# A fourteen-stage transformer block on one Trainium2 core: token-major first tiles behind nine layer norms, a bias table through DRAM, and one tile for three small projections

## What is computed

| j | 0 | 1 | 2 | 3 | 4 | 5 | 6 | 7 | 8 | 9 | 10 | 11 | 12 | 13 |
|---|---|---|---|---|---|---|---|---|---|---|---|---|---|---|
| f | even | cross | ffn | odd | cross | ffn | ffn | merge | cross | ffn | ffn | merge | cross | ffn |

## Time and profile before

### The profile page before, as it was taken

One profiled execution on the slowest core, in us unless ns is written; L12 is line 12 of the kernel. 1 busy time (PEld: TensorE's weight loads), 2 busy tenths in 40 slices (PEclk: granted clock), 3 DMA queues, 4 the chain that ended last, 5 costly groups with the idle time before them and its releaser, 6 DMA issues. The chain is left out here.

```text
span 2473.5 us, 38184 instructions
## 1 busy us (share of the span) xinstructions
PE 2344.4 (95%) x16097; PEld 2138.9 (86%) x16097; DVE 1470.3 (59%) x1648; ACT 1091.4 (44%) x1238; POOL 126.6 (5%) x178
## 2 busy tenths in 40 slices
PE   8989999998999999999999998999999999998998
PEld 7868899877888988988887987998998987896996
DVE  6466555478756555554765676556555655676554
ACT  3444444344444434432555444434443365444442
POOL 2140000000000000000011000000000012000000
PEclk9899999999999999997999999999998899999999
DMA  8535355553545555555442563655555443464653
GB/s 255 162 94 196 125 190 188 187 161 103 188 136 185 191 187 187 189 187 165 138 135 81 187 228 120 196 187 183 194 190 185 136 128 114 129 217 134 203 189 118
DMA packets 329402, 412.59 MB, mean 167 GB/s; under 512 B 15189, under 2 KB 261137, under 8 KB 329105
## 3 DMA queue, kind: packets, MB, share of 16 engines
q1 hardware_dynamic: 320160, 377.71, 47.0%
q0 software_dynamic: 9072, 32.44, 4.3%
HBM read 405.13 MB, written 4.98 MB: 166 GB/s over the span
## 5 line engine op out<-in xcount | busy, mean ns | idle before, releaser
L1365 DVE TENSOR_TENSOR wl<-raw,wh 128x2048 fp32r<-128x2048 f32 (+2 forms) x379 | 827.5, 2188 | 708.1 <-ACT wh L955 622.8
L324 PE MATMUL bank<-xl,wh 128*128 128x256 f32 x3440 | 976.1, 284 | 10.4 <-issue 9.7
L324 PE MATMUL bank<-xh,wl 128*128 128x256 f32 x3440 | 966.5, 281 | 0.0
L324 PE MATMUL bank<-xh,wh 128*128 128x256 f32 x3440 | 965.7, 281 | 0.0
L955 ACT ACTIVATE wh<-raw 128x2048 fp32r<-128x2048 f32 (+2 forms) x379 | 688.8, 1820 | 449.7 <-PE bank L324 428.6
L324 PEld LDWEIGHTS bank<-xl,wh 128*128 128x128 f32 x3440 | 660.5, 192 | 25.0 <-issue 24.2
L324 PEld LDWEIGHTS bank<-xh,wh 128*128 128x128 f32 x3440 | 661.6, 192 | 0.0
L324 PEld LDWEIGHTS bank<-xh,wl 128*128 128x128 f32 x3440 | 660.3, 192 | 1.0 <-issue 0.2
L324 PE MATMUL bank<-wl,hh 128*128 128x512 f32 x528 | 205.9, 390 | 0.0
L324 PE MATMUL bank<-wh,hh 128*128 128x512 f32 x528 | 205.5, 389 | 0.0
L324 PE MATMUL bank<-wh,hl 128*128 128x512 f32 x528 | 205.4, 389 | 0.0
(11 more groups left out here) (305 smaller groups left out, 2774.5 us busy)
## 6 DMA issues: line engine op xcount, KB each, us to landing
raw<-in_ffn_w_in SPq DMA_DIRECT2D x88, 1024.0 KB, 5.1
raw<-in_w_mix_in SPq DMA_DIRECT2D x56, 1024.0 KB, 5.3
raw<-in_ffn_w_gu SPq DMA_DIRECT2D x44, 1024.0 KB, 5.1
raw<-in_ffn_w_out SPq DMA_DIRECT2D x40, 1024.0 KB, 5.1
raw<-in_ffn_w_down SPq DMA_DIRECT2D x20, 1024.0 KB, 5.1
raw<-in_mem_wkv SPq DMA_DIRECT2D x16, 1024.0 KB, 5.8
raw<-in_even_w_in SPq DMA_DIRECT2D x14, 1024.0 KB, 6.4
raw<-in_odd_w_in SPq DMA_DIRECT2D x12, 1024.0 KB, 5.2
```

The lines of the kernel that those rows point to most:

```text
L324: ins = pe.transpose(o, a, b) if transpose else pe.matmul(o, a, b, start=start, stop=stop)
L1365: dve.tensor_tensor(wl[:, t % PARTS, 0:nk * w], raw_tile(t), wh[:, t % PARTS, 0:nk * w].bitcast(F32), ALU.subtract)\
```

## The change

1. At the nine stage changes the next stage opens token-major. Its first three weight tiles (two for odd) are ordered ahead in the weight stream and split into memory outside the ring: `front` has its own, `side` is `oh`/`ol`, `back` is eight chunks of `hh`/`hl`, `mem` and `note` lie over memory that is free in a cross stage. `enter` makes block 0's products from them, then transposes block 1, then makes block 1's products from the same tiles. `x_to_T` of block 0 stands now before the last three matmuls of t=1, not before the last twelve.
2. ffn: the three tiles are gate columns 0 to 255, up columns 0 to 255, and gate and up 256 to 383 together. The hidden values are token-major there and get six transposes (`hid_T`) behind the first tile of the ring; nine pairs and a `last` tile (128 gate and 128 up columns) follow, so the count of tiles stays 22.
3. odd: the first half of the values comes first, and no longer behind the third rotary tile. merge: `vs` (two tiles) comes first, then one tile of 200 columns, which is `ckv`, `ik` and `iw` together; `ik` is copied and transposed by two matmuls; the earlier `ckv`, `ik`, `iw` and the later `vs` projections are gone.
4. even: one matmul of 8 output rows, one copy, a DMA of 16 KB to `row_d`, and later one DMA from DRAM to DRAM that broadcasts it to the 2 MB.
5. GpSimd's constant loads of odd and merge wait now for a bank of the new first products.

```diff
+    def part_of(n, low):
+        _, nk, w, slot, _ = weight_tiles[n]
+        if slot == "front":
+            return (front_h, front_l)[low][:, 0:nk * w]
...
+        return (wh, wl)[low][:, slot, 0:nk * w]
...
+        def order(pieces, nk, slot=None):
             n = len(weight_tiles)
             w = sum(piece.shape[-1] for piece in pieces)
-            weight_tiles.append((pieces, nk, w))
+            if slot is None:
+                before = len(ring) - PARTS + 1
+                slot = len(ring) % PARTS
+                ring.append(n)
+            else:
+                before = free_after.get(slot, 0)
+            weight_tiles.append((pieces, nk, w, slot, before))
+            return n
...
             held = 0 if cross_after(j) else min(PARTS, len(steps))
+            enters = j + 1 < LAST and not cross_after(j)
+            early, late = entry_slots(j) if enters else ([], [])
+            tiles = []
             for half, k0 in steps[:len(steps) - held]:
                 if need:
                     need(min(k0 + 4, kc))
                 y_step(j, W, half, k0, kc, sh, sl)
+                if (half, k0) in ((0, 4), (0, 12)) and enters:
+                    tiles.append(order_entry(j + 1, len(tiles), early.pop(0)))
                 if half == 0 and k0 + 4 >= kc and cross_after(j):
                     mem_start[j + 1] = len(halves)
                     mem_to_T(j + 1)
-            tiles = []
+            if enters and kc == HC:
+                free_after["back"] = len(ring) - 1
+                if early:
+                    tiles.append(order_entry(j + 1, len(tiles), early.pop(0)))
+            held_tiles = []
             for half, k0 in steps[len(steps) - held:]:
                 if need:
                     need(min(k0 + 4, kc))
-                tiles.append(y_tile(j, W, half, k0, kc))
-                y_products(j, 0, half, k0, kc, sh, sl, tiles[-1])
+                held_tiles.append(y_tile(j, W, half, k0, kc))
+                while early or late and (half, k0) == steps[-1]:
+                    tiles.append(order_entry(j + 1, len(tiles), (early or late).pop(0)))
+                if (half, k0) == steps[-1]:
+                    if enters:
+                        entry_last[j + 1] = tiles[-1]
+                y_products(j, 0, half, k0, kc, sh, sl, held_tiles[-1])
             for i, (half, k0) in enumerate(steps[len(steps) - held:]):
-                if i == held - 1 and j + 1 < LAST:
+                ks = list(range(k0, min(k0 + 4, kc)))
+                if i == held - 1 and enters:
+                    y_products(j, 1, half, k0, kc, sh, sl, held_tiles[i], ks[:-1])
                     x_to_T(j + 1, [0])
-                y_products(j, 1, half, k0, kc, sh, sl, tiles[i])
+                    ks = ks[-1:]
+                y_products(j, 1, half, k0, kc, sh, sl, held_tiles[i], ks)
                 owed[0] += 1
             if cross_after(j):
                 cross_kv(j + 1)
-            elif j + 1 < LAST:
-                x_to_T(j + 1, [1])
+            elif enters:
+                enter(j + 1, tiles)
...
+        def entry_slots(j):
+            n = {"ffn": 3, "odd": 2, "merge": 3}[SUB[j + 1][0]]
+            return (["front", "side", "back"][:n], []) if SUB[j][0] == "ffn" else (["mem", "note"], ["front"])
+        def order_entry(i, n, slot):
+            kind, blk, layer, which = SUB[i]
+            if kind == "ffn":
+                w, _ = ffn_weights(blk, layer, which)
+                pieces = ([w[:, 0:S]], [w[:, FFN:FFN + S]], [w[:, S:S + P], w[:, FFN + S:FFN + S + P]])[n]
+                return order(pieces, KC, slot)
+            w = A["odd_w_in"][0] if kind == "odd" else A["w_mix_in_2"][layer]
+            c0 = 2048 if kind == "odd" else 2248
+            if n < 2:
+                return order([w[512 * n:512 * n + 512, c0:c0 + 512]], 4, slot)
+            return order([w[:, 512:640], w[:, 1152:1224]], KC, slot)
+        def block_products(name, c0, tile, t, k0, n, first, last, full):
+            h, l = tile
+            o = ps[where[name][0]]
+            tok = slice(t * P, t * P + P)
+            width = h.shape[-1]
+            for k in range(n):
+                three(o[:, c0:c0 + width], xh[:, k0 + k, tok], xl[:, k0 + k, tok], h[:, k, :], l[:, k, :],
+                      first and k == 0, last and k == n - 1, name if full and k == n - 1 else None)
+        def enter(i, tiles):
+            kind, _, layer, _ = SUB[i]
+            views = []
+            for t in range(TB):
+                if t == 1:
+                    x_to_T(i, [1])
+                await_parts()
+                for m, n in enumerate(tiles):
+                    if t == 0:
+                        views.append(arrived(n))
+                    tile = views[m]
+                    if kind == "ffn":
+                        name = ("gu", i, t) if m < 2 else ("gv", i, t)
+                        if m != 1:
+                            take(name, "acc", frees=2)
+                        block_products(name, m % 2 * S, tile, t, 0, KC, True, True, m > 0)
+                    elif m < 2:
+                        name = ("dv", t, 0) if kind == "odd" else ("vs", layer, t)
+                        if m == 0:
+                            take(name, "acc")
+                        block_products(name, 0, tile, t, 4 * m, 4, m == 0, m == 1, m == 1)
+                    else:
+                        take(("ckv", layer, t))
+                        block_products(("ckv", layer, t), 0, tile, t, 0, KC, True, True, True)
+            for slot in ("front", "side"):
+                free_after[slot] = len(ring) + 1
...
-            for q in range(HC // 2):
-                proj_T(("gate", j, q), [wgu[:, q * S:q * S + S]], KC, xh, xl, entry=q == 0)
-                proj_T(("up", j, q), [wgu[:, FFN + q * S:FFN + q * S + S]], KC, xh, xl)
+            c0 = S + P
+            for q in range(PAIRS):
+                proj_T(("gate", j, q), [wgu[:, c0 + q * S:c0 + q * S + S]], KC, xh, xl)
+                if q == 0:
+                    await_read(("gu", j, 0), ("gu", j, 1), ("gv", j, 0), ("gv", j, 1))
+                    for i, ms in enumerate(((0, 1), (2,))):
+                        o = take(("hid_T", j, i))
+                        for m in ms:
+                            for t in range(TB):
+                                mm(o[:, m % 2 * S + t * P:m % 2 * S + t * P + P], hid[:, t, m * P:m * P + P], ident[:, :],
+                                   True, True, ("hid_T", j, i) if t == 1 and m == ms[-1] else None, transpose=True)
+                        parts(("hid_T", j, i))
+                proj_T(("up", j, q), [wgu[:, FFN + c0 + q * S:FFN + c0 + q * S + S]], KC, xh, xl)
                 parts(("hid", j, q), in_bank=False)
-            out_proj(j, wdown, HC, hh, hl, need=lambda k: await_parts(base + (k + 1) // 2))
+            proj_T(("last", j), [wgu[:, FFN - P:FFN], wgu[:, 2 * FFN - P:2 * FFN]], KC, xh, xl, frees=2)
+            parts(("hid", j, PAIRS), in_bank=False)
+            out_proj(j, wdown, HC, hh, hl, need=lambda k: await_parts(base + (1 + k // 2 if k < HC else 3 + PAIRS)))
...
-            for hd in range(8):
-                o = take(("tab", hd), "acc")
-                mm(o[:, :], brel0[:, hd:hd + 1].broadcast_to([BUCKETS, P]), boneh[0:BUCKETS, :], True, True,
-                   ("tab", hd))
+            o = take("tab", "acc")
+            mm(o[0:8, :], brel0[:, :], boneh[0:BUCKETS, :], True, True, "tab")
...
-            proj_N([("ckv", l_, t) for t in range(TB)], W, 512, P, KC, xh, xl, entry=True)
-            h, l = weights([W[:, 1152:1216], W[:, 1152:1216], W[:, 1216:1224]], KC)
-            o = take(("ik", l_))
-            for k in range(KC):
-                three(o[:, 0:S], h[:, k, 0:P], l[:, k, 0:P], xh[:, k, :], xl[:, k, :], k == 0, k == KC - 1,
-                      ("ik", l_) if k == KC - 1 else None)
-            o = take(("iw", l_))
-            for t in range(TB):
-                for k in range(KC):
-                    tok = slice(t * P, t * P + P)
-                    three(o[:, t * 8:t * 8 + 8], xh[:, k, tok], xl[:, k, tok], h[:, k, P:P + 8], l[:, k, P:P + 8],
-                          k == 0, k == KC - 1, ("iw", l_) if t == 1 and k == KC - 1 else None)
-            owed[0] += 1
             for n in range(2):
                 proj_T(("iq", l_, n), [W[:, 640 + n * S:640 + n * S + S]], KC, xh, xl)
+                if n == 0:
+                    o = take(("ik", l_))
+                    for t in range(TB):
+                        pe.wait_ge(sig("index_keys"), 2 * l_ + t + 1)
+                        mm(o[:, t * P:t * P + P], z[:, 1, t * P:t * P + P], ident[:, :], True, True,
+                           ("ik", l_) if t == 1 else None, transpose=True)
             pe.wait_ge(sig("ckv_normed"), 2 * (l_ + 1))
...
-                if pair == 0:
-                    proj_N([("vs", l_, t) for t in range(TB)], W, 2248, 512, KC, xh, xl)
-                else:
...
+                if j + 1 in entry_last:
```

(20 more changed lines are left out.)

191 lines of the change are left out of this document (123 added, 68 removed).

## The result

| | before | changed |
|---|---|---|
| median of four runs | 2471.05 us | 2408.53 us |
| lowest, highest | 2469.42, 2477.91 | 2407.53, 2411.29 |
| profiled execution, its span | 2475.34, 2473.5 | 2411.29, 2409.5 |
| mean granted clock | 0.966 | 0.987 |

The ratio of the runs is 0.9744, 95% interval 0.9723 to 0.9764: faster by 2.6%. The forecast was 2403, range 2388 to 2430, and it is the forecast's own case that came, no rival. Against the profiled execution the forecast was 67.7 us less; it became 64.0 less.

What follows compares the result with a forecast made beforehand. TensorE's own work and its standing times, with half clock behind them, were taken as the bound. Terms 9.0 + 8.2 + 0 + 5.5 + 36.8 + 10.2 − 2.0 = 67.7 us off 2470.6 gave 2403, range 2388 to 2430.

Steps and rivals of the forecast that it cites:

- The cover: Stage openings: block 0's products, 8.1 us at ffn to ffn, hide block 1's norm with 3.5 us in reserve.
- The clock: Stage openings: two gaps of some 1.7 us each replace one long gap and keep full clock; half a microsecond charged.
- rival 1: All nine openings: clock falls as before, 2.9 us per opening, 26 less gain, 2429 us; chance 0.14.
- A: Two ffn to ffn openings: 5.0 us gained each, 0.5 taken off for a ring tile's split, 9.0 for both.
- B: Two openings from cross with two halves to ffn: 4.1 us gained each, 8.2 for both.
- C: Two openings from cross with one half to ffn: extra splits delay the softmax, earlier products offset it; 0, bounds ±4 each.
- D: The ffn to odd opening, with two tiles of values: 6.4 us less 0.9 for dip and stall, 5.5 gained.
- E: Two ffn to merge openings and merges: fewer products, 200-column ones priced like 256; 18.4 us each, 36.8 gained.
- rival 3: Merge: a 200-column product costs more than one of 256, up to 22 us in all, 2425 us; chance 0.04.
- Rival 4: Merge: the chain behind z sets the pace, so 17.8 us of the merge gain is lost, 2421 us; chance 0.03.
- F: Even stage: bias table matmuls fall from 11.4 us to 1.1, a gain of 10.2.
- Rival 5: All nine openings: late early-tile splits stand before the norm, 62 us plus 31 of half clock, 2496 us; chance 0.02.

Runs made afterwards that it cites:

- experiment 2: Changed kernel with block 1's transposes ahead of block 0's products, so nothing covers block 1's norm: 2488.78 us, ratio 1.0046 to the kernel before.
- Experiment 4: Changed kernel with the third early tile of ffn to ffn and ffn to merge openings ordered behind the first held tile: 2407.99 us.
- Experiment 6: Changed kernel with the first two early tiles split sooner in the two cross stages with one half: 2402.66 us.
- experiment 1: Kernel before with only the even stage's bias table change (one matmul, one copy, row store, later broadcast): 2459.29 us, ratio 0.9945.
- experiment 3: Changed kernel with all early tiles ordered behind the stage's last held tile: 2446.72 us, 41.6 more than the unaltered changed kernel.

## Why the prediction was right, and where it was not

**What bounds it**: right. The gain came from TensorE's standing time, the half clock behind it, and TensorE's own work in merge and even.

**The cover**: right in mechanism and in size. I gave block 1's norm 3.5 us of reserve at ffn to ffn; its x was ready 3.8 us before the transposes. Taking the cover away costs about 8 us an opening (6.5 at ffn 6), where 7.1 was expected.

**The clock**: rival 1 (0.14, 2429) did not come. The rows of the kernel before had a gap of 2.38 us that left the clock at 1.00, and the new ones are 0.99 and 1.69. The Trainium skill, TensorE: Matmul & The Clock Gate, section HAM oscillation, says that a kernel whose TensorE waits for several microseconds between groups of matmuls is throttled again at each wait; by the trace that is so for the single gap of 4.35 us (clock 0.50 behind it in experiment 2), and not for the two shorter ones (1.00). Between these lengths a gap alone does not decide: in the changed kernel the 2.45 us in merge 7 left the clock at 1.00, and 2.46 us at the same place in merge 11 were followed by 0.57 over 4 us. The prediction also took the half clock as 6.8 us long behind every opening. That is so at the ffn stages; in merge 7 of the kernel before it was 0.50 from 1136 to 1153 and again from 1156.5 to 1166.6.

**A**: mis-sized, 4.4 against 9.0. The opening gave 4.0 and not 5.0, and the term "0.5 for a first ring tile whose split waits" was 1.8, at another place: in the output projection ahead of the opening, where the third early tile waits for its borrowed memory with the ring behind it. Experiment 4 shows both the place and the price.

**B**: 3.0 in ffn 5 against 4.1; the 7.8 in ffn 2 holds 4.3 of a slower spacing that fell on the kernel before by chance.

**C**: the step "0 after a small dip" failed. The softmax slipped 4.4 on VectorE, as forecast, and the cross stages grew by 4.0, under the 5.8 of the sum; but the opening behind gave 3.0 and not the 5.9 that the sum had set against it. So the pair costs 1.0 us, which is within the −4 to +4 each that I had as bounds, and in the profile 5.4 more in ffn 9, by the spacing and 3.4 us of half clock. Experiment 6 shows that the 4.0 were the two splits, half clock in the softmax included, and free to avoid: I had the two idle times of VectorE (2.96 and 2.43 us) in the trace and did not ask whether the splits could stand there.

**D, E**: 4.7 for 5.5, 36.7 for 36.8. The latter is partly luck, as the merges' lengths differ by some 5 us between profiles: 312.0 and 311.7 in experiment 1, whose merges are those of the kernel before (317.6 and 316.4). Against these the gain would be 15 and 13. Most of the difference is the clock of the first 36 us, 0.62 against 0.76 in the windows above. I had read E off the profile with the lower clock, and it was measured against the same profile, so the two had to agree in that. Which of the two is usual for this kernel stays open: experiment 1's profile is its fastest run. The price of 200 columns was right: rival 3 is out, and so is the 0.086 us that I had estimated for 200 columns from the Trainium skill, TensorE: Matmul & The Clock Gate, section Back-to-back issue gap; the trace has 0.111 us for 200 columns and 0.113 for 256. Rival 4 is out too: the chain behind z shows only as a wait of 2.45 us.

**F**: too small, 10.2 against 15.4 in the two profiles and 11.7 by the mean. I priced the removed matmuls and not the half clock that they left behind them, 1.5 us; the rest is the stage's own difference between executions, whose cause is open.

**Rival 5**: the mechanism exists (experiment 3, 41.6 us), the early order keeps it away. Its size was put at 93.

The errors cancelled in part: A and C came out 12.5 us worse than forecast, B and F 7.8 better. The time was nearer than its terms, and that is luck.

## What to carry to other kernels

Work that covers a wait must be independent of what is waited for and ready before it: here both the order of the products (about 73 us by the lengths of the stages) and the early splits (41 us) were needed, and without the first nothing was left of the whole change. When a tile gets memory of its own, ask which line it stands in: one that waits for its memory holds up all that are behind it on the same engines. Place such splits in idle time that the trace shows on that engine, not where a count of tiles looked ahead happens to put them; and compare stage by stage, since medians hid an effect of 6 us that four stages each showed to a hundredth. And take more than one profile of the kernel before: a stage of it can be 5 us longer or shorter by its clock or its spacing alone.

## What the runs showed of the hardware that was not expected

- At the same granted clock of 1.00 a stream of float32 products of 256 columns runs at one of two spacings, 0.113 or 0.118 us (797 or 767 in 90 us). In an ffn stage one of them lasts some 120 us; elsewhere it changes within a stage, behind other matmuls. What chooses it stays open.
- TensorE's clock was at 0.50 from 60.80 to 74.40 us in the kernel before, in a stretch in which the records have it busy throughout, most of it on 8 broadcast matmuls of 32 rows and 512 columns.
- Gaps of like length at like places left the clock at 1.00 in one merge (2.45 us) and were followed by half clock in the other (2.46 us), and the first 36 us of merge 7, the same code in the kernel before and in experiment 1, got 0.62 of the clock in one profile and 0.76 in the other.
- Products of 200 columns (0.111 us) cost what those of 256 do (0.113) in this float32 form; those of 8 and of 128 had the like price at the lower clock.
